# A feed-forward block's gates and values with the tokens on partitions: quarters of 512 columns, and transposes of their products

## The reference

```python
h = rms_norm(x, g_ffn_pre[layer])
gate, up = jnp.split(h @ w_gate_up[layer], 2, axis=-1)
x = x + rms_norm((jax.nn.silu(gate) * up) @ w_down[layer], g_ffn_post[layer])
```

## Time and profile before

| | before |
|---|---|
| median of 3 runs | 2654.79 us |
| lowest and highest | 2652.17 and 2655.65 us |
| span of the profiled execution | 2653.3 us |
| TensorE, VectorE, ScalarE busy | 2636.2, 1871.7, 1510.4 us |
| weight traffic | 488 MB read, 186 GB/s over the span |

### The profile page before, as it was taken

One profiled execution on the slowest core, in us unless ns is written; L12 is line 12 of the kernel. 1 busy time (PEld: TensorE's weight loads), 2 busy tenths in 40 slices (PEclk: granted clock), 3 DMA queues, 4 the chain that ended last, 5 costly groups with the idle time before them and its releaser, 6 DMA issues.

```text
span 2653.3 us, 38713 instructions
## 1 busy us (share of the span) xinstructions
PE 2636.2 (99%) x13730; PEld 2236.2 (84%) x13730; DVE 1871.7 (71%) x3539; ACT 1510.4 (57%) x3006; POOL 38.8 (1%) x56
## 2 busy tenths in 40 slices
PE   9999999999999999999999999999999999999998
PEld 7888888888888888888887888988888888888887
DVE  7877566465876577657767678666688758866885
ACT  7775555455655455545557665554566546655654
POOL 0000000000000000000003000000000000000000
PEclk9999999999999999999999999999999999999999
DMA  8455547666666666665665555545656666666565
GB/s 282 147 167 162 181 152 238 192 208 197 184 187 191 206 204 187 193 191 186 188 188 178 173 161 187 156 149 162 186 180 192 193 192 186 190 190 192 187 192 160
DMA packets 136817, 493.09 MB, mean 186 GB/s; under 512 B 15704, under 2 KB 16216, under 8 KB 135856
## 3 DMA queue, kind: packets, MB, share of 16 engines
q1 hardware_dynamic: 134064, 480.04, 57.8%
q0 software_dynamic: 2272, 10.31, 1.2%
q10 hardware_dynamic: 288, 0.26, 0.0%
HBM read 488.44 MB, written 4.21 MB: 186 GB/s over the span
## 4 chain that ended last, share of the span: by engine, by line
PE 98%; DVE 1%; ACT 0%; issue 0%; DMA 0%; DVEq 0%; SPq 0%; ACTq 0%
PE bank L614 97%; PE bank L653 0%; DVE lo L1627 0%; DVE X L1630 0%; PE bank L729 0%; DVE arena L1627 0%; DVE XS L1630 0%; DMA raw<-in_ws_mix 0%; ACT sq_t L1181 0%; PE bank L867 0%; PE bank L901 0%; ACT hi L1076 0%; PE bank L677 0%; PE bank L694 0%; PE bank L807 0%
## 5 line engine op out<-in xcount | busy, mean ns | idle before, releaser
L1627 DVE TENSOR_TENSOR lo<-raw,hi 128x512 fp32r<-128x512 f32 x1804 | 1233.2, 690 | 659.7 <-ACT hi L1076 548.2
L1076 ACT CAST hi<-raw 128x512 fp32r<-128x512 f32 x1804 | 1098.0, 619 | 696.8 <-PE bank L614 678.1
L614 PE MATMUL bank<-XS,hi 128*128 128x512 f32 x3632 | 1000.2, 396 | 1.6 <-DVE XS L1630 1.6
L614 PEld LDWEIGHTS bank<-XS,hi 128*128 128x128 f32 x3632 | 620.8, 189 | 90.8 <-issue 4.0
L614 PEld LDWEIGHTS bank<-XS,lo 128*128 128x128 f32 x3632 | 557.0, 189 | 77.1
L614 PE MATMUL bank<-XS,lo 128*128 128x256 f32 x3632 | 578.5, 281 | 0.0
L614 PE MATMUL bank<-hi,HS 128*128 128x512 f32 x1952 | 545.6, 391 | 0.0
L614 PE MATMUL bank<-hi,XS 128*128 128x512 f32 x1600 | 448.3, 394 | 1.7 <-DVE XS L1630 1.1
L614 PEld LDWEIGHTS bank<-hi,HS 128*128 128x128 f32 x1952 | 364.0, 188 | 75.5 <-ACT hi L1076 1.3
L614 PEld LDWEIGHTS bank<-hi,XS 128*128 128x128 f32 x1600 | 296.8, 189 | 66.0 <-ACT hi L1076 4.4
L614 PE MATMUL bank<-lo,HS 128*128 128x512 f32 x976 | 321.6, 389 | 0.0
(11 more groups left out here) (198 smaller groups left out, 985.5 us busy)
## 6 DMA issues: line engine op xcount, KB each, us to landing
raw<-in_ws_ffn SPq DMA_DIRECT2D x528, 512.0 KB, 3.5
raw<-in_ws_mix SPq DMA_DIRECT2D x338, 512.0 KB, 3.6
raw<-in_ws_ple SPq DMA_DIRECT2D x35, 512.0 KB, 4.1
arena<-in_gains POOLq DMA_DIRECT2D x4, 1024.0 KB, 5.9
X<-in_xt POOLq DMA_DIRECT2D x1, 2048.0 KB, 13.1
t5rows<-t5row POOLq DMA_DIRECT2D x8, 256.0 KB, 5.1
out<-arena SPq DMA_DIRECT2D x8, 256.0 KB, 2.5
X<-in_x SPq DMA_DIRECT2D x7, 256.0 KB, 5.3
```

Of the source, the lines that this page charges most:

```text
L614: return eng.matmul(o, l, r, start=start, stop=stop, skip_group_check=True)
L1076: eng.copy(hi[:, b % SPL, :], raw[:, u % RAW, part * BW:(part + 1) * BW]).then_inc(halved.next(b), 1)
L1627: return eng.tensor_tensor(o, a, b, op)
```

## The change

The gates and values become quarters: `gate1` and `value1` are now 11 groups each of 64 tiles (16 batches), in banks (0, 2) and (1, 7). The root of the norm is then a number for each partition (`roots_of`), used as a scale. ScalarE takes the sigmoid straight from the bank into `u_t` (two areas of 1024 columns, `hid`), VectorE multiplies by the gates and then by the values, 512 columns at a time. The products lie with tokens on partitions, and the down-projection needs them the other way round. So behind each value quarter TensorE transposes eight tiles of 128x128 into banks 5 and 6, and ScalarE and VectorE split two chunks at a time into `HS`. The parts of the down-projection are 16, 16 and 12 chunks. Nothing is spread over partitions for this norm any more.

```diff
+FOURS = [(0, 4), (4, 8), (8, 11)]
...
+    def gated_ffn(up, down):
+        out = []
+        for p, (a, b) in enumerate(FOURS):
+            for q in range(a, b):
+                out += [quarter("gate1", q, up, q), quarter("value1", q, up, q, key=lambda k: NF + k)]
+            out += [quarter("down1", (q, p), down, q, BT * a, BT * b) for q in range(4)]
+        return out
...
-    return [("ws_mix1", mix1 + proj(0, 1)), ("ws_ffn1", ffn("1", "w_gate_up", "w_down")), ("ws_ple", ple),
+    return [("ws_mix1", mix1 + proj(0, 1)), ("ws_ffn1", gated_ffn("w_gate_up", "w_down")), ("ws_ple", ple),
...
-TILES_OF = {"hf": 1, "hq": 2, "gate1": 2, "value1": 1,
+TILES_OF = {"hf": 1, "hq": 2,
...
-         "down1": [(3, 4), (5, 6), (3, 4), (2, 7)], "ple": [(2, 7), (0, 1), (2, 7), (0, 1)],
+         "gate1": [(0, 2)] * 11, "value1": [(1, 7)] * 11, "down1": [(3, 4), (5, 6), (3, 4), (2, 7)], "ple": [(2, 7), (0, 1), (2, 7), (0, 1)],
...
+        def hid(q):
+
+            return u_t[:, BT * (q % 2):BT * (q % 2) + BT, :].rearrange("p c t -> p (c t)").rearrange("p (m n) -> p m n", m=2)
...
+            def hidden(g):
+
+                yield 4
+                for k in range(2):
+                    b = 5 + k
+                    clear(b)
+                    for m in range(2):
+                        on.wait_ge(t_dve, (g.g, m))
+                        for x in range(2):
+                            c = 2 * k + x
+                            t = eng.transpose(bank[b][:, T * x + P * m:T * x + P * m + P],
+                                              hid(g.q)[:, m, c * P:(c + 1) * P], ident)
+                    t.then_inc(crossed.next(("hidden", g.q, k)), 1)
+                    free[b] = [(ready, ("hidden1", BT * g.q + 2 * k))]
...
-            for name in ("mix", "ffn", "mix2", "ffn2"):
+            for name in ("mix", "mix2", "ffn2"):
...
-            def value1(g):
-                copy(g)
-                yield after_gate(g)
-                on.wait_ge(combined, (g.g, "times"))
-                i = g.i
-                if i >= 16:
-                    on.wait_ge(gemm, ("half", by["down1", (3, (i - 16) // 15)].g, 1))
-                eng.copy(HS[:, i % 16, 0:T], tile(g.u[0])).then_inc(upper.next(("hidden1", i)), 1)
+            def quarter_of_gate1(g):
+                on.wait_ge(n_dve, ("ffn", "root"))
+                if g.q > 1:
+                    on.wait_ge(crossed, ("hidden", g.q - 2, 1))
+                for m in range(2):
+                    if m:
+                        yield 1
+                    on.wait_ge(gemm, ("half", g.g, m))
+                    eng.activation(hid(g.q)[:, m, :], bank[g.banks[m]], ACT.Sigmoid, scale=roots_of("ffn")[:, m:m + 1]).then_inc(
+                        t_act.next((g.g, m)), 1)
+
+            def hidden(g):
+
+                yield 5
+                for k in range(2):
+                    c = BT * g.q + 2 * k
+                    on.wait_ge(crossed, ("hidden", g.q, k))
+                    if g.q > 3:
+                        on.wait_ge(gemm, ("half", by["down1", (3, g.q // 4 - 1)].g, 1))
+                    eng.copy(HS[:, c % 16:c % 16 + 2, 0:T], bank[5 + k].rearrange("p (c t) -> p c t", c=2)).then_inc(
+                        upper.next(("hidden1", c), ("hidden1", c + 1)), 1)
...
-            def gate1(g):
-                u = take(g.u[0])
-                yield from scaled_to(g, u)
-                yield after_root(g) + 1
-                on.wait_ge(curved, g.g)
-                tt(u, u, tile(g.u[1]), ALU.mult).then_inc(combined.next((g.g, 1)), 1)
-
-            def value1(g):
-                v = take(g.u[0])
-                yield from scaled_to(g, v)
-                yield after_gate(g)
-                gate = by["gate1", g.i]
-                on.wait_ge(combined, (gate.g, 1))
-                on.wait_ge(scaled, g.g)
-                tt(v, v, tile(gate.u[0]), ALU.mult).then_inc(combined.next((gate.g, 0), (g.g, "times")), 1)
-                yield after_gate(g) + 1
-                lower(HS[:, g.i % 16, :], v, ("hidden1", g.i))
+            def quarter_of_gate1(g):
+
+                for m in range(2):
+                    if m:
+                        yield 1
+                    on.wait_ge(t_act, (g.g, m))
+                    part = hid(g.q)[:, m, :]
+                    stt(part, bank[g.banks[m]], roots_of("ffn")[:, m:m + 1], part, ALU.mult, ALU.mult).then_inc(
+                        t_dve.next((g.g, m)), 1)
+
+            def quarter_of_value1(g):
+
+                gate = by["gate1", g.q]
+                for m in range(2):
+                    if m:
+                        yield 1
+                    on.wait_ge(t_dve, (gate.g, m))
+                    on.wait_ge(gemm, ("half", g.g, m))
+                    part = hid(g.q)[:, m, :]
+                    stt(part, bank[g.banks[m]], roots_of("ffn")[:, m:m + 1], part, ALU.mult, ALU.mult).then_inc(
+                        t_dve.next((g.g, m)), 1)
+
+            def hidden(g):
+
+                yield 5
+                for k in range(2):
+                    c = BT * g.q + 2 * k
+                    on.wait_ge(upper, ("hidden1", c))
+                    tt(HS[:, c % 16:c % 16 + 2, T:2 * T], bank[5 + k].rearrange("p (c t) -> p c t", c=2),
+                       HS[:, c % 16:c % 16 + 2, 0:T].bitcast(F32), ALU.subtract).then_inc(
+                        ready.next(("hidden1", c), ("hidden1", c + 1)), 1)
...
-                if name == "ple":
+                if name in ("ffn", "ple"):
```

More of the change, by code:

```diff
@@ L917, in tensor @@
                     agenda.at(g.last, merge(g))
+                elif g.kind == "value1":
+                    agenda.at(g.last, hidden(g))
                 elif g.kind == "misc":
@@ L1061, in program @@
                 if k == 0:
-                    by_part |= {"aq": (ready, ("aq", g.i)), "uv": (ready, ("mixed", g.i)),
-                                "value1": (ready, ("hidden1", g.i))}
+                    by_part |= {"aq": (ready, ("aq", g.i)), "uv": (ready, ("mixed", g.i))}
                 elif g.kind == "value2":
@@ L1548, in scalar @@
             quarters = {"wout": quarter_of_wout, "down1": quarter_of_down1, "ple": quarter_of_ple,
-                        "o1": quarter_of_x, "down2": quarter_of_x, "hi": quarter_of_values, "bv": quarter_of_values, "qkv": quarter_of_heads,
+                        "gate1": quarter_of_gate1, "o1": quarter_of_x, "down2": quarter_of_x, "hi": quarter_of_values, "bv": quarter_of_values, "qkv": quarter_of_heads,
                         "ga": quarter_of_gates, "hg": quarter_of_gates, "gb": quarter_of_gates}
-            steps = {"hf": hf, "hq": sigmoid, "gate1": sigmoid,
-                     "value1": value1, "gate2": convolved, "value2": convolved,
+            steps = {"hf": hf, "hq": sigmoid, "gate2": convolved, "value2": convolved,
                      "ql": place, "misc": misc, "kv": kv, "aq": upper_half, "uv": upper_half}
@@ L2390, in forget @@
                     lower(HS[:, 8 + h, :], bank[b][:, 0:T], ("mixed", 8 + h))
-            steps = {"hf": hf, "hq": hq, "gate1": gate1, "value1": value1, "misc": misc, "iq": iq, "kv": kv, "aq": aq,
+            steps = {"hf": hf, "hq": hq, "misc": misc, "iq": iq, "kv": kv, "aq": aq,
                      "bq": bq, "bk": bk, "uv": uv, "gate2": convolved, "value2": convolved}
             quarters = {"wout": quarter_of_wout, "down1": quarter_of_down1, "ple": quarter_of_ple,
+                        "gate1": quarter_of_gate1, "value1": quarter_of_value1,
                         "o0": quarter_of_x, "o1": quarter_of_x, "down2": quarter_of_x, "qkv": quarter_of_heads,
@@ L2412, in vector @@
                 agenda.at(by["wb", q].last, merged(by["wb", q]))
+            for q in range(11):
+                agenda.at(by["value1", q].last, hidden(by["value1", q]))
             agenda.at(by["wout", 1].last + 1, p_split(0))
```

## The result

The changed kernel takes 2650.42 us (median of 14 runs, 2648.59 to 2651.65), the one before in the same sessions 2655.12 us (14 runs, 2652.17 to 2657.04): 4.7 us less, a ratio of 0.9982 with a 95% interval of 0.9974 to 0.9990. The forecast was 2650.1 us and a gain of 4.7. The interval leaves out a ratio of 1, and the gain lies inside the 0.2% that were called "the same" beforehand. In microseconds the interval runs from 2.7 to 6.9, so that the medians meet the forecast to a tenth is luck; what can be held against its terms is the stage in the trace.

A forecast was written before the change was run, and what follows sets the result against it. TensorE was taken to bound the kernel, its time the sum of what it issues. Terms: -14.6 + 9.9 - 0.4 + 0.4 = -4.7 us, from 2654.79 to 2650.1 us; range 2646.5 to 2654.0.

The forecast's parts named there:

- The batches: Gate and value batches change form: 336 at the steady distance save 0.0428 us each, 14.4 us; 14.6 us in all.
- My third rival: Gate and value batches save only the fixed part of two matmuls, 9.4 us; sum +0.5, 2655.3 us; chance 0.05.
- The transposes: Eleven new bursts of eight transposes, one behind each value quarter, cost 0.90 us each, 9.9 us.
- The cheap: Rival: bursts cost 0.79 us each and bank 2 is never waited for; sum -6.3, 2648.5 us; chance 0.17.
- the dear rival: New bursts cost the merge's 1.37 us each, 15.1 us; sum +0.5, 2655.3 us; chance 0.06.
- The root and the opening: No spreading of the stage's root saves TensorE 0.4 us; the first 16 batches save 0.2 us.
- VectorE and ScalarE at nothing: VectorE's gate and value work falls from 130 to 48 us, ScalarE's copies too; counted as nothing for the time.
- The bank: Next gate quarter waits 0.4 us for bank 2 after down-projection part 1, not after part 0.
- The slow rival: Weights late at 22 more quarter ends; with 0.69 us exposed at each, +10.5 us, 2665.3 us; chance 0.05.

The follow-up runs named there:

- The cut: Changed kernel with each low matmul of a gate or value batch cut into two of 256 columns: 2664.32 us, ratio 1.0037.
- the widened kernels: Kernel before the change with the low matmuls of its gates and values 512 columns wide instead of 256: 2798.2 us, ratio 1.0533.
- the run with the load put back: Changed kernel with the low half of every fourth batch of the stage made twice on VectorE: 2651.64 us, ratio 0.9988.

## Why the prediction was right

**The batches.** 336 x 0.0428 = 14.4 us was the largest term. The new stage keeps 1.3603 us per batch, the number taken from w_out's quarters. What I did not know is why: I gave the mix and the form one price together. The cut and the widened kernels show that it is the number and mixture of the matmuls' lengths. My third rival had the right mechanism for two thirds of it (0.027 of 0.043) and was wrong in leaving out the rest, which the rows held already.

**The transposes.** 0.90 us per burst stood in the earlier trace rows and stands in each of the eleven. The cheap and the dear rival are both out, the cheap one because the full 0.90 is paid eleven times and bank 2 is waited for. Against the dear one the prediction argued with the plain matmuls of the merge, and called the count the same. That count is not the same: each of the four plain matmuls is two instructions in the trace, so the merge's burst has twelve. The earlier trace rows shows six, the other six are

```profile
572.04 0.38 PE L694 MATMUL bank<-cst,X 128*128 128x128 f32 x2
572.26 0.61 PE L614 MATMUL bank<-cst,X 128*128 128x128 f32 x4
```

and 1.37 / 12 = 0.114 us each is about the 0.90 / 8 = 0.113 of the new bursts.

**The root and the opening.** The ten batches with transposes ahead of them take 666.22 to 682.29, 16.07 us against 16.15: 0.008 each, as ple had it. With the root's 0.4 us and the batches the sum gives -14.6 - 0.4 + 9.9 + 0.5 = -4.6, and the stage shows -4.58.

**VectorE and ScalarE at nothing.** Held by the run with the load put back, with a limit I had not named: it holds behind the opening. VectorE's relief itself was put at 130 - 48 = 82 us and is 72, which changes nothing in the sum. Nor does the remark that DMA moves its bytes 0.4% sooner, a figure that no term gives: 4.7 of the stage's 743 us are 0.6%.

**The bank.** Predicted as one wait of 0.4 us behind part 1 and none behind part 0; found as 0.52 us behind part 1 and none behind part 0. The wait is VectorE's addition, which reads bank 2 until 1196.34:

```profile
1195.66 0.68 DVE L1670 TENSOR_TENSOR arena<-arena,bank 128x512 f32<-128x512 f32 x1
```

The second pair of matmuls starts 1196.40 - 1195.56 = 0.84 us behind the first instead of 0.45, so the wait is 0.39 as predicted, and the idle entry shows 0.23 of it because the first pair is still busy at the beginning. The other 0.12 went into that pair itself, 0.57 us to the next start instead of 0.45, which the prediction did not have.

**The slow rival.** I had named the weights' low halves as what would be late. They are at a gate end; at a value end it is the product ahead of the burst, and I had that time from hg, where the product ends 1.1 us ahead of the burst although VectorE does twice the work.

## What to carry to other kernels

When TensorE is busy throughout, price a change by start-to-start distances of whole batches, taken over many batches of each form (120 and 60 here), and check the sum against the stage's length and not the span's. Equal columns are not equal time: fewer and longer matmuls of one length are cheaper, but a layout that needs 128x128 transposes afterwards pays 0.11 us for each, and here two thirds of what the form saved went into them. Slack has to be read at the wait that ends last at each kind of place; the same engine had 5 us at one end and 2 us at the next. A forecast that is right in its terms can still be worth little: the whole gain here is 0.18%.

## What I had not expected of the hardware

Matmuls with a weight load of their own each cost the columns at 2.4 GHz plus 0.0133 us, for 256 and for 512 columns (0.120 and 0.2267 us). The Trainium skill (page "TensorE: Matmul & The Clock Gate", section "Back-to-back issue gap") has about 2.5 ns there, for isolated matmuls, and for a stream with weight loads about 131 ns per matmul of 512 columns; the prediction worked with the first figure and did not say that it is for isolated ones. Neither agrees with the 226.7 ns here, and the measurement decides. Taking turns between four of 512 and four of 256 costs another 0.013 us per eight (1.400 instead of 1.387).

A pause of 3.51 us on TensorE was followed by work at the lower clock level in nine cases of ten (1.81 us for four matmuls instead of about 1.0 behind a burst, granted clock 0.83 over the 10 us around it), and so was a pause of 2.20 us (granted clock 0.69 in a window behind it), but none of 0.8. Such pauses then cost more than their own length.
